# Conditioning sums of one stage gathered in the rows of one PSUM bank, with one copy and one turn per stage

## What is computed

```python
sc, scc = jax.nn.silu(c), jax.nn.silu(c_ctx)
...
    mod_l = jnp.split((sc @ w_ada[l] + b_ada[l])[:, None, :], ADA_CHUNKS, axis=-1)
    mod_c = jnp.split((scc @ w_ada[l] + b_ada[l])[None, None, :], ADA_CHUNKS, axis=-1)
    h = ffn_half_step(h, mod_l[0], mod_l[1], mod_l[2], g_ffn1[l], w_ffn1_in[l], w_ffn1_out[l])
    ...
    hn = modulate(rms_norm(h, g_mix[l]), mod_l[3], mod_l[4])
```

## Time and profile before

| | before |
|---|---|
| timed runs, median (lowest to highest) | 3289.75 us (3288.23 to 3290.12) |
| profiled execution: span from first to last instruction | 3286.1 us |
| profiled execution: own time | not given on the page apart from the span |
| PE busy | 3207.4 us, 98% of the span |
| DVE busy | 1911.6 us, 58% |
| ACT busy | 631.9 us, 19% |
| mean granted TensorE clock | 0.997 |

### The profile page before, as it was taken

The page is one execution under the profiler, slowest core; times in us unless marked ns, Lnnn a source line. Parts: engine busy times, 40 slices in busy tenths (PEclk is TensorE's granted clock), DMA queues, the critical chain, the costliest instruction groups (busy, mean ns, idle before and its releaser), DMA issues.

```text
span 3286.1 us, 41038 instructions
## 1 busy us (share of the span) xinstructions
PE 3207.4 (98%) x15462; PEld 2463.8 (75%) x15462; DVE 1911.6 (58%) x3783; ACT 631.9 (19%) x1327; POOL 161.0 (5%) x307
## 2 busy tenths in 40 slices
PE   7999999999999999999999999999999999999999
PEld 5888865548888878888667888544488887756888
DVE  5887842638887787778353624555285684654100
ACT  2000023421000020000342002355210000254100
POOL 0000000000000000000000100000000000000000
PEclk9999999999999999999999999999999999999999
DMA  7554522114554345544324853311142332331543
GB/s 275 164 173 148 173 71 67 43 52 160 173 164 155 124 147 167 161 158 137 101 75 136 290 166 126 119 52 58 38 168 90 122 122 77 132 101 39 167 153 102
DMA packets 115189, 422.76 MB, mean 129 GB/s; under 512 B 13040, under 2 KB 16368, under 8 KB 112976
## 3 DMA queue, kind: packets, MB, share of 16 engines
q1 hardware_dynamic: 75232, 265.32, 25.0%
q0 software_dynamic: 39504, 154.77, 14.7%
q10 hardware_dynamic: 288, 0.36, 0.0%
HBM read 418.29 MB, written 1.31 MB: 128 GB/s over the span
## 4 chain that ended last, share of the span: by engine, by line
PE 93%; DVE 3%; ACT 2%; issue 1%; DMA 1%; DVEq 0%; ACTq 0%; SPq 0%
PE PS L930 30%; PE PS L982 18%; PE PS L875 11%; PE PS L1457 6%; PE PS L1038 6%; PE PS L1432 3%; PE PS L1360 2%; PE PS L1003 2%; PE PS L1278 2%; PE PS L1109 1%; PE PS L1523 1%; PE PS L1216 1%; PE PS L779 1%; PE PS L770 1%; PE PS L1070 1%
## 5 line engine op out<-in xcount | busy, mean ns | idle before, releaser
L875 PE MATMUL PS<-xn,ring 128*128 128x256 f32 (+1 forms) x1504 | 372.0, 408 | 2.8 <-ACT xn L1726 2.3
L875 PEld LDWEIGHTS PS<-xn,ring 128*128 128x128 f32 x1504 | 283.9, 190 | 89.0 <-issue 45.9
L930 PE MATMUL PS<-xn,ring 128*128 128x256 f32 x1312 | 301.4, 383 | 3.7 <-ACT xn L1717 3.7
L930 PEld LDWEIGHTS PS<-xn,ring 128*128 128x128 f32 x1312 | 246.8, 191 | 56.5 <-issue 19.1
L1457 PE MATMUL PS<-xn,arena 128*128 128x512 f32 (+1 forms) x640 | 256.3, 533 | 0.0
L982 PE MATMUL PS<-xn,ring 128*128 128x256 f32 x752 | 223.7, 379 | 0.0
L2237 DVE SCALAR_TENSOR_TENSOR mix<-arena,cond,mix 128x1024 f32<-128x1024 f32 x182 | 222.6, 1278 | 0.0
L982 PE MATMUL PS<-arena,ring 128*128 128x256 f32 x784 | 202.1, 380 | 0.2
L982 PE MATMUL PS<-xn 128*128 128x256 f32 x752 | 193.0, 379 | 0.0
L1038 PE MATMUL PS<-arena,ring 128*128 (+1 forms) x864 | 186.8, 379 | 0.0
L2406 DVE SCALAR_TENSOR_TENSOR h<-PS,gate,h 128x256 f32<-128x256 f32 x64 | 26.8, 478 | 266.8 <-PE PS L1038 179.7
(11 more groups left out here) (355 smaller groups left out, 4953.5 us busy)
## 6 DMA issues: line engine op xcount, KB each, us to landing
ring<-stream SPq DMA_DIRECT2D x500, 512.0 KB, 3.7
arena<-fed_w POOLq DMA_DIRECT2D x200, 512.0 KB, 4.0
arena<-pair_m POOLq DMA_DIRECT2D x8, 1536.0 KB, 7.1
mix<-fed_w POOLq DMA_DIRECT2D x24, 512.0 KB, 3.9
arena<-pair_n POOLq DMA_DIRECT2D x8, 1024.0 KB, 5.2
mix<-gate_sums POOLq DMA_DIRECT2D x32, 256.0 KB, 4.4
mix<-na_bias POOLq DMA_DIRECT2D x8, 512.0 KB, 4.0
h<-xT SPq DMA_DIRECT2D x1, 1024.0 KB, 6.5
```

Source lines behind the costliest of these rows:

```text
L875: m = pe.matmul(PS[:, bank, 0:tokens], ring[:, s, k * P:(k + 1) * P], xn[:, k, 0:tokens], start=k == 0, stop=k == DC - 1)
L930: m = pe.matmul(out, weights, moving, start=k == 0, stop=k == 3)
```

## The change

The blocks of one stage (the 5, 4 or 1 of an `up7` or `swiglu` phase, the 2 of a `norm` phase) share one PSUM bank. The weights of `fed_sum` are no longer ones but a 32-column window of a new constant `row_sel` that has a single column of ones; the window is placed so that block b writes its sum to row b of each quarter and adds zero to the other rows. Only block 0 starts the accumulation; the others add to it. After the stage's last block there is one copy of the bank by ACT, one turn by PE, now four plain 128x128 transposes, and one addition for each block by DVE, which reads its row's 16 columns out of the 512. The first copy, the turn and the adds of the earlier blocks thus wait for the last block's place in the stage. In a `norm` phase the second sum goes to the first's bank (5, not 7), and the copy ahead of chunk 1 goes. `adarow2` shrinks to `adarow` (512 columns less), and the constants grow by 55 columns, which come with the first constants' load at the start.

```diff
-for _name, _w in (("ident", P), ("ones", P), ("ada_sel", 8), ("fed_sel", 8),
+for _name, _w in (("ident", P), ("ones", P), ("ada_sel", 8), ("row_sel", 63),
...
-            def fed_sum(ph, block, bank, free):
-                pe.wait_ge(ada_done, free)
+            def fed_sum(ph, block, bank):
+                if block == 0:
+                    pe.wait_ge(ada_done, ph.at.ada)
                 pe.wait_ge(fed_used, DC * (ph.at.fed + block + 1))
                 sums = fed_places(ph.at.fed + block)[0][(ph.at.fed + block) % 2]
                 for q in range(4):
-                    m = pe.matmul(PS[32 * q:32 * q + 32, bank, :], ones[:, 0:32],
-                                  sums[q // 2][:, (q % 2) * 512:(q % 2 + 1) * 512], start=True, stop=True)
+                    m = pe.matmul(PS[32 * q:32 * q + 32, bank, :], const("row_sel")[:, 31 - block:63 - block],
+                                  sums[q // 2][:, (q % 2) * 512:(q % 2 + 1) * 512], start=block == 0, stop=True,
+                                  skip_group_check=True)
                 m.then_inc(ada_mm, 1)
-            def fed_turn(ph, block, bank, row, free):
-                pe.wait_ge(ada_done, free)
-                pe.wait_ge(ada_row, ph.at.ada + block + 1)
+            def fed_turn(ph, bank):
+                pe.wait_ge(ada_row, ph.at.turn + 1)
                 for c in range(4):
-                    m = pe.matmul(PS[:, bank, 8 * c:8 * c + 8], adarow2[:, row, c * P:(c + 1) * P], const("fed_sel"),
-                                  start=True, stop=True)
+                    m = pe.transpose(PS[:, bank, c * P:(c + 1) * P], adarow[:, c * P:(c + 1) * P], ident)
                 m.then_inc(ada_turned, 1)
-            def norm_turns(ph):
-                fed_turn(ph, 0, 6, 0, ph.at.ada)
-                fed_turn(ph, 1, 5, 1, ph.at.ada)
...
-                    norm_turns(last)
+                    fed_turn(last, 6)
...
                     block = fed_block(ph, j)
                     if block is not None:
-                        fed_sum(ph, block, FED_BANK, ph.at.ada + block)
+                        fed_sum(ph, block, FED_BANK)
                     for name in PRODUCTS:
                         product(j, name)
-                        if name == "P7" and block is not None:
-                            fed_turn(ph, block, FED_BANK, 0, ph.at.ada + block)
+                        if name == "P7" and block is not None and block + 1 == ph.ada:
+                            fed_turn(ph, FED_BANK)
...
-                if ph.ada and c in (1, 3):
-                    ada_copy(ph, c // 2, bank=(5, 7)[c // 2], row=c // 2)
+                if ph.ada and c == 3:
+                    ada_copy(ph, 1, bank=5)
...
+            def fed_adds(ph, bank):
+                ob, _ = COLS["b_ada"]
+                dve.wait_ge(ada_turned, ph.at.turn)
+                for n in range(ph.ada):
+                    at = ph.at.ada - 1 + n
+                    pair = slice(0, 2) if at < ADA_AT[2] else slice(2, 4)
+                    out = mod[:, 32 * at:32 * at + 32].rearrange("p (h c j) -> p h c j", h=2, c=4)[:, :, :, pair]
+                    bias = par[:, ob + DC * at:ob + DC * at + DC].rearrange("p (h c j) -> p h c j", h=2, j=1)
+                    tt(out, fed_bank_row(bank, n), bias.broadcast_to([P, 2, 4, 2]), ALU.add).then_inc(ada_done, 1)
```

More of the change, by code:

```diff
@@ L150 @@
 FIRST_CONSTS = CONSTS["rot1"][0]
-COUNTED = ("unit", "acc", "evac", "silu", "glu", "out", "h", "sq", "sum", "std", "rstd", "scaled", "nout", "ada",
+COUNTED = ("unit", "acc", "evac", "silu", "glu", "out", "h", "sq", "sum", "std", "rstd", "scaled", "nout", "ada", "turn",
            "sg", "up", "head", "headtile", "gates", "pair", "pairtile", "values",
@@ L170, in make_plan @@
     count["evac"] = 4
-    count["ada"] = 1
+    count["ada"] = count["turn"] = 1
     plan = []
@@ L187, in norm @@
         return phase("norm", what=what, chunks=chunks, tokens=tokens, pieces=pieces, shifted=shifted, layer=layer,
-                     ada=ada, adds=dict(ada=ada, fed=ada, sq=chunks, sum=1, std=1, rstd=1, scaled=4 if wide else n, nout=n if shifted else 0))
+                     ada=ada, adds=dict(ada=ada, turn=min(ada, 1), fed=ada, sq=chunks, sum=1, std=1, rstd=1, scaled=4 if wide else n, nout=n if shifted else 0))
     def swiglu(layer, which, tokens):
@@ L195, in swiglu @@
             phase("up7", layer=layer, which=which, tokens=tokens, ada=ada, n=PAIRS,
-                  adds=dict(unit=U_SWIGLU, fed=ada, silu=PAIRS, glu=PAIRS, ada=ada, prep=PAIRS, comb=4, fold=PAIRS,
+                  adds=dict(unit=U_SWIGLU, fed=ada, silu=PAIRS, glu=PAIRS, ada=ada, turn=min(ada, 1), prep=PAIRS, comb=4, fold=PAIRS,
                             folding=PAIRS))
@@ L201, in swiglu @@
         phase("swiglu", layer=layer, which=which, tokens=tokens, ada=ada,
-              adds=dict(unit=U_SWIGLU, acc=U_SWIGLU, silu=PAIRS, glu=PAIRS, ada=ada, fed=ada))
+              adds=dict(unit=U_SWIGLU, acc=U_SWIGLU, silu=PAIRS, glu=PAIRS, ada=ada, turn=min(ada, 1), fed=ada))
         phase("down", layer=layer, which=which, tokens=tokens, n=U_DOWN, src="hidden", glu_end=count["glu"],
               adds=dict(unit=U_DOWN, out=4 * U_DOWN, h=DC * halves))
-    phase("ada", blocks=2, adds=dict(unit=2 * DC, ada=2))
+    phase("ada", blocks=2, adds=dict(unit=2 * DC, ada=2, turn=2))
     for l in range(2):
@@ L237, in make_plan @@
             phase("up7", layer=l, which="mlp", tokens=tokens, n=MC // 2, ada=ada,
-                  adds=dict(unit=MC, ada=ada, fed=ada, glu=MC // 2, prep=MC // 2, comb=4, fold=MC // 2))
+                  adds=dict(unit=MC, ada=ada, turn=min(ada, 1), fed=ada, glu=MC // 2, prep=MC // 2, comb=4, fold=MC // 2))
             phase("down7", layer=l, which="mlp", tokens=tokens, n=MC, src="hidden", glu_end=count["glu"],
@@ L279, in build @@
         rstd = sb("rstd", [P, 3, P])
-        adarow2 = sb("adarow2", [P, 2, 512])
-        adarow = adarow2[:, 0, :]
+        adarow = sb("adarow", [P, 512])[:, :]
         fed_more = sb("fed_more", [P, UNIT])
@@ L570, in fed_block, with fed_bank_row @@
             return block if part == 3 and 0 <= block < ph.ada else None
+        def fed_bank_row(bank, block):
+            return PS[:, bank, :].rearrange("p (c j h r) -> p h c j r", c=4, j=2, h=2)[:, :, :, :, block]
         def fed_places(block):
@@ L1658, in _, with ada_copy @@
                            ACT.Silu).then_inc(cond_ready, 1)
-            def ada_copy(ph, block, i=0, bank=ADA_BANKS[0], row=0):
+            def ada_copy(ph, block, i=0, bank=ADA_BANKS[0]):
                 act.wait_ge(ada_mm, i + (ph.at.ada + block))
-                act.activation(adarow2[:, row, :], PS[:, bank, :], ACT.Copy).then_inc(ada_row, 1)
+                act.activation(adarow, PS[:, bank, :], ACT.Copy).then_inc(ada_row, 1)
             def norm_copy(ph, c):
-                if ph.ada and c in (1, 3):
-                    ada_copy(ph, c // 2, bank=(5, 7)[c // 2], row=c // 2)
+                if ph.ada and c == 3:
+                    ada_copy(ph, 1, bank=5)
             def ada(ph):
@@ L1741, in up7 @@
                     block = fed_block(ph, j)
-                    if block is not None:
+                    if block is not None and block + 1 == ph.ada:
                         ada_copy(ph, block, bank=FED_BANK)
@@ L2209, in swiglu @@
                     block = fed_block(ph, j)
-                    if block is not None:
-                        ada_add(ph, block, bank=FED_BANK)
+                    if block is not None and block + 1 == ph.ada:
+                        fed_adds(ph, FED_BANK)
                     if 1 <= j <= 4 * ph.ada:
@@ L2904, in head_selectors, with row_selector @@
     return nope, rope, pe
-def fed_selector():
-    m = np.zeros((P, 8), np.float32)
-    for q in range(4):
-        for j in (q // 2, q // 2 + 2):
-            m[32 * q, 4 * (q % 2) + j] = 1.0
+def row_selector():
+    m = np.zeros((P, 63), np.float32)
+    m[:, 31] = 1.0
     return m
```

17 lines of the change are left out of this document (7 added, 10 removed).

## The result

| | before | after |
|---|---|---|
| runs, median (lowest to highest) | 3289.92 us (3288.23 to 3290.12, 4 runs) | 3268.33 us (3264.53 to 3271.21, 4 runs) |
| ratio, 95% interval | | 0.9933 (0.9921 to 0.9945) |
| span of the profiled execution | 3286.1 us | 3262.6 us |
| its own time | 3288.23 us | 3264.53 us |
| mean granted TensorE clock | 0.997 | 0.998 |

The change takes 21.6 us off the median, 0.66%; 3269.1 had been forecast. The two profiled executions are each the fastest of their kernel here; they lie 23.5 us of span apart.

A forecast was written before the change was run, and what follows sets the result against it. PE was taken to bound the kernel nearly everywhere, with ACT's copies counting in the norms. Terms 12.15 + 1.85 + 6.6 = 20.6 us off 3289.75 gave 3269.1 us, range 3265.5 to 3276.0.

The forecast's parts named there:

- PE sets the end: Nearly everywhere, time taken from PE's queue comes off the end; PE is busy 98% of the span.
- The turns that go: In `up7`, `swiglu` and the mlp, 15 of 20 turns drop at 0.81 us each: 12.15 us, all on the path.
- The turns that stay: The last turn of five stages becomes four transposes, 0.44 us in place of 0.81: 1.85 us saved.
- The second rival: In the remaining turns a transpose costs its whole 0.273 us; nine turns lose 5.9 us, giving 3275.0; chance 0.05.
- The sums at nothing: The 28 sums stay at 1.0 us each; adding to the bank instead of overwriting it costs nothing.
- The first rival: In the sums, the four quarters run one behind the other: 70 us more, 3339; chance 0.02.
- The norms, 6.6: Four norm phases save 3 x 1.74 + 1.42 = 6.6 us, by one turn of transposes for two and one ACT copy fewer.
- The third rival: The norm phases give nothing back because ACT or DVE hold the chunks: 14.0 us left, 3275.8; chance 0.07.
- The adds covered, the copies free in `up7`: Five adds, 0.95 us, fit DVE's 3.43 us wait ending an `up7`; fewer ACT copies there are worth nothing.
- DVE paces `up7`: In `up7`, what PE saves is waited away, leaving the norms' 6.6 and `swiglu`'s 2.8 us: 3280.3; chance 0.03.
- The clock: More norms may fall to 1.2 GHz, 1.5 us each; three such stretches make 4.5 us, 3273.6; chance 0.06.
- a sign of being wrong: In the new profile, more stretches at half clock would show the prediction wrong.

The follow-up runs named there:

- changed, once more: The changed kernel with no edit, run again for its spread and a second profile: 3267.65 us, ratio 0.9936 to the kernel before.
- every block turned: Against the kernel before, only the turn changed to four transposes; each block keeps its own sum, copy, turn and add: 3278.89 us, ratio 0.9968.
- turned by matmuls: The changed kernel with its nine turns made by plain f32 matmuls against the identity, not transposes: 3272.21 us, ratio 0.9947 to before.
- ACT's copy kept: The changed kernel with an ACT instruction of a copy's length put back ahead of chunk 1 in the norms: 3269.60 us, ratio 0.9941 to before.
- norm's turn later: The changed kernel with the norm phases' remaining copy, turn and adds moved later, the turn behind the first unit: 3268.34 us, ratio 0.9938 to before.
- the last experiment: The changed kernel with each of DVE's 28 adds made three times, each behind the one before: 3267.27 us, one run.

## Why the prediction was right

Point by point, by its own steps.

- **PE sets the end.** Right. Each microsecond taken from PE in `up7`, `swiglu` and the mlp comes off the stretch, and adding 0.45 a turn by matmuls puts it back.
- **The turns that go, 12.15 us.** Mis-sized: 15 x 0.89 = 13.35. The distance from the turn to the next start missed the 0.08 us by which the next group was longer. The row that would have shown it is the start of the group after that, 312.22.
- **The turns that stay, 1.85.** The 0.44 was right to 0.01 us wherever it was read; the 0.81 was short in the same way: 5 x 0.45 = 2.25. The sentence that reads the skill's length of a transpose as its cost in the queue would have taken about 6 us off the sum; the nine turns at 0.44 decide against it. The second rival, a transpose at its whole 0.273, has fallen: what overlaps there overlaps here.
- **The sums at nothing.** Right: 592 ns a record, 1.00 us a sum. The first rival has fallen.
- **The norms, 6.6.** 7.0 measured: 1.82, 1.79, 1.54, 1.82 against 1.74, 1.74, 1.42, 1.74. What was missing is again mostly the 0.08 behind the turns, four times, 0.32 of the 0.4. The step to the seventh chunk came at 5.90, inside its 5.9 to 6.0, and the share of ACT's copy is 0.38 to 0.45 where 0.48 was taken. The third rival has fallen.
- **The adds covered, the copies free in `up7`.** Right, with more room than was claimed: adds of five times the length fit in, and with all copies back a block's four steps are only the transposes' 0.45 us shorter.
- **DVE paces `up7`**, the fifth rival: it has fallen, 49.54 us for four steps with DVE 40.83 busy.

So the terms come to 22.6 us, 2.0 more than the 20.6 of the forecast. That the median was met within 0.8 us is partly luck, since the medians moved less than the terms:

| kernel | its terms against before | its median against before |
|---|---|---|
| changed, first runs | 22.6 | 21.6 |
| changed, once more | 22.6 | 20.9 |
| every block turned | 12.8 | 9.6 |
| turned by matmuls | 18.9 | 16.3 |
| ACT's copy kept | 20.9 | 18.9 |
| norm's turn later | 22.6 | 20.2 |

Each falls short by 1.0 to 3.2 us. **The clock**, the fourth rival, is the likely taker. The profiles show where the difference lies. Cut at the same 40 landmarks and at the first fed sum, all of them agree, with before or with what was read above, to 0.03 us but in six places, and in these the clock's levels mostly lie differently from profile to profile.

The first is the start, up to the first fed sum: against before 0.6 us less in the changed kernel's first profile, 0.9 more in the repeated one, and 2.4, 2.7 and 2.5 more in the next three. In those three the first conditioning sums begin at the lower level, with records of 1.06 us like the longest of the earlier trace rows, where before they begin at 0.592. The same 32 records, before and in the run turned by matmuls:

```profile
17.78 3.79 PE L757 MATMUL PS<-ring,cond 128*32 128x512 f32 x32
```

```profile
19.04 5.58 PE L760 MATMUL PS<-ring,cond 128*32 128x512 f32 x32
```

Part of the start is also the wait for weights told above. Stretches at the lower level are found in every profile, also in that of before, mostly near the same spots of the program: at 25 to 40 us, and around 1720, 2770 and 3000 us. But one spot, in the attention of layer 2, is at full clock in the profile of before, and at half in five of the seven profiles with a change. The stretch there, in the changed kernel's first profile and, at the same place of the program, in that of before:

```profile
2302.90:2306.30 3.40, 3.40 (x11) 2.12 (x10) 2.46 (x5) 1.28 (x6) 0.00 (x0) 0.50 0.02 5
```

```profile
2325.10:2328.50 3.40, 3.40 (x13) 1.42 (x11) 2.41 (x5) 2.27 (x7) 0.00 (x0) 1.00 0.00 0
```

PE's timelines, after and then before:

```profile
2303.31 1.91 PE L1001 MATMUL PS<-arena,ring 128*128 128x512 f32 x2
2305.02 1.06 PE L1521 MATMUL PS<-cst,probs 128*128 128x128 f32 x4
```

```profile
2325.25 1.02 PE L1003 MATMUL PS<-arena,ring 128*128 128x512 f32 x2
2326.25 0.63 PE L1523 MATMUL PS<-cst,probs 128*128 128x128 f32 x4
```

The same two records take 1.71 us from start to start and not 1.00; the phase as a whole is 363.1 us where it is 361.6 in before and in the repeated run. A second spot, near 667 us, is at half clock in four of the seven and adds 0.6 to 0.9 us. What runs there is untouched by the change. Whether the change draws the clock down more often, by the moments at which its phases now fall, stays **open**: there is one profile of before, and a median cannot say it. The forecast had named more stretches at half clock as a sign of being wrong. The sign decides nothing here: by its record of the clock the profile of before spends 21.8 us at the lower level, the first of the changed kernel 10.8, and the other six 21.6 to 27.5. The lowest runs of all are 3287.53 for before (of 21) and 3264.53 for the changed kernel (of 9): 23.0 apart, near the terms' 22.6, though the second is the execution with the 10.8. The forecast's fourth rival had named 1.5 us a stretch and the norms touched by the change as the place. The size was right for the dense spot; the place was mostly not: one such norm, ahead of the third `up7`, fell in one profile and cost 0.28 us.

## What to carry to other kernels

Count the pairs of weight load and matmul of a small piece of PE work before its columns: a turn of f32 data by a matmul with a few selector columns costs as much as one over all 128, and a transpose costs half. Ask for the cheaper form and for fewer of them, and price each alone: here the form alone was worth 12.8 us, fewer turns alone 18.9, both 22.6. Price a piece on a saturated engine from its start to a start two groups on, less the group's usual length, because part of its cost is paid by its successor. In a phase that runs at another engine's pace, what that engine does between its pieces is part of the path, to its full length.

## What the runs showed of the hardware

- An f32 load and matmul with 128x128 weights cost 0.11 us from start to start with 8 columns as with 128, at full granted clock, and 0.216 with 256; four f32 transposes cost 0.44 us in all while the record of each is 0.273 us long. The Trainium skill, TensorE: Matmul & The Clock Gate, section Part 4: PE-mode transpose, has the length of the record, about 275 ns, and the trace agrees; as a price in the queue it would be 2.5 times too high.
- Undisturbed stretches that hold the same work repeat to 0.02 us out of 411, in four profiles on two chips. Differences of a few hundredths of a us between kernels can be read from profiles stretch by stretch where the medians, with a spread of up to 6.7 us, can't tell 2 us.
- Sums that add to a bank in four column quarters cost what sums that overwrite it cost, 592 ns a record.
- Adds of 128x16 that don't depend on each other overlap: the record of one is 0.165 us long, five in a row last 0.50 us; the fifteen of the last experiment, three in order for each block, last 2.59.
